# Second layers: TensorE multiplies the mask into banks that are overwritten later, ahead of the fourth scores and ahead of the first convolution input

## What is computed

```python
y_conv = conv_branch(a, a_glu, ...) * silu(z_conv)   # y = a * sigmoid(a_glu); causal depthwise conv, 31 taps;
                                                     # layer norm, silu, 256x256 product
y_mla  = mla_branch(c_q, c_kv, k_rope, ...) * silu(z_mla)   # 8 heads: q, k of 96, v of 64, causal softmax
y_sg   = sgu_branch(u, v, ...) * silu(z_sg)          # gelu(u) * (masked 128x128 mixing of normed gelu(v))
x = x + concat(rms(y_conv), rms(y_mla), rms(y_sg)) @ w_out
```

## Time and profile before

| | |
|---|---|
| median of 3 executions | 1483.45 us (1482.19 to 1486.08) |
| profiled execution | 1483.63 us, of which the span from first to last instruction is 1481.9 us |
| TensorE busy | 1428.2 us, 96% of the span |
| VectorE, ScalarE busy | 986.7 us (67%), 826.7 us (56%) |
| mean granted TensorE clock | 0.988 of full speed |

### The profile page before, as it was taken

One profiled execution on the slowest core, in us unless ns is written; L12 is line 12 of the kernel. 1 busy time (PEld: TensorE's weight loads), 2 busy tenths in 40 slices (PEclk: granted clock), 3 DMA queues, 4 the chain that ended last, 5 costly groups with the idle time before them and its releaser, 6 DMA issues.

```text
span 1481.9 us, 18967 instructions
## 1 busy us (share of the span) xinstructions
PE 1428.2 (96%) x7631; PEld 1203.0 (81%) x7631; DVE 986.7 (67%) x1468; ACT 826.7 (56%) x1337; POOL 44.9 (3%) x72
## 2 busy tenths in 40 slices
PE   7999999999999999989999999999999989899988
PEld 6877888888778888857888888778888878788877
DVE  6665656556766565676765656657656589868984
ACT  6775434445745354464454356765534468856883
POOL 3000000000000000000000000000000020112010
PEclk9999999999999999999999999999999999999999
DMA  9433545554335455423445554424455454424430
GB/s 300 170 114 137 204 171 202 196 171 170 115 125 210 177 190 208 167 90 114 171 175 211 182 186 169 170 105 179 171 201 197 170 156 139 170 101 158 150 115 29
DMA packets 119508, 242.12 MB, mean 163 GB/s; under 512 B 3083, under 2 KB 48957, under 8 KB 119421
## 3 DMA queue, kind: packets, MB, share of 16 engines
q1 hardware_dynamic: 117648, 237.25, 45.1%
q0 software_dynamic: 1408, 3.52, 1.0%
q10 hardware_dynamic: 364, 0.13, 0.0%
HBM read 239.84 MB, written 1.05 MB: 163 GB/s over the span
## 4 chain that ended last, share of the span: by engine, by line
PE 85%; DVE 8%; ACT 5%; issue 1%; DMA 1%; ACTq 0%; DVEq 0%
PE pair L1183 17%; PE pair L1185 17%; PE pair L1184 17%; PE pair L1573 16%; PE pair L1575 8%; PE pair L1338 3%; DVE wlo L1728 2%; PE pair L1281 2%; DVE yacc L2123 2%; PE pair L1359 1%; PE pair L1389 1%; ACT whi L706 1%; PE pair L1344 1%; ACT xparts L747 1%; PE pair L1377 1%
## 5 line engine op out<-in xcount | busy, mean ns | idle before, releaser
L1728 DVE TENSOR_TENSOR wlo<-raw,whi 128x2048 fp32r<-128x2048 f32 (+2 forms) x240 | 504.6, 2132 | 77.4 <-ACT whi L706 76.4
L706 ACT ACTIVATE whi<-raw 128x2048 fp32r<-128x2048 f32 (+2 forms) x238 | 414.5, 1783 | 57.7 <-DMA raw<-in_mlp_w_down 30.5
L1573 PE MATMUL pair<-xparts,whi 128*128 128x512 f32 x1024 | 260.7, 393 | 2.0 <-DVE xparts L1764 1.8
L1183 PE MATMUL pair<-whi,ahi 128*128 128x512 f32 x640 | 253.4, 396 | 1.4 <-DVE alo L1764 1.1
L1184 PE MATMUL pair<-wlo,ahi 128*128 128x512 f32 x640 | 249.9, 390 | 0.0
L1185 PE MATMUL pair<-whi,alo 128*128 128x512 f32 x640 | 249.7, 390 | 0.0
L1183 PE MATMUL pair<-whi,xparts 128*128 128x512 f32 (+2 forms) x624 | 242.2, 388 | 4.5 <-issue 2.6
L1185 PE MATMUL pair<-whi,xparts 128*128 128x512 f32 (+2 forms) x624 | 236.3, 379 | 0.0
L1184 PE MATMUL pair<-wlo,xparts 128*128 128x512 f32 (+2 forms) x624 | 235.7, 378 | 0.0
L1573 PEld LDWEIGHTS pair<-xparts,whi 128*128 128x128 f32 x1024 | 184.1, 189 | 38.6 <-DVE xparts L1764 4.5
L976 ACT ACTIVATE qkv<-pair 128x512 f32<-128x512 f32 x64 | 38.2, 597 | 271.2 <-PE pair L1575 271.2
(11 more groups left out here) (251 smaller groups left out, 1416.1 us busy)
## 6 DMA issues: line engine op xcount, KB each, us to landing
raw<-in_mlp_w_up SPq DMA_DIRECT2D x32, 2048.0 KB, 8.9
raw<-in_mlp_w_down SPq DMA_DIRECT2D x32, 2048.0 KB, 7.5
raw<-in_diff_w_in SPq DMA_DIRECT2D x20, 1024.0 KB, 7.2
raw<-in_w_in SPq DMA_DIRECT2D x10, 2048.0 KB, 8.1
raw<-in_moba_w_in SPq DMA_DIRECT2D x12, 1024.0 KB, 6.1
raw<-in_diff_w_out SPq DMA_DIRECT2D x4, 2048.0 KB, 7.7
raw<-in_w_uq SPq DMA_DIRECT2D x4, 1152.0 KB, 5.5
raw<-in_moba_w_out SPq DMA_DIRECT2D x2, 2048.0 KB, 7.8
```

Of the source, the lines that this page charges most:

```text
L706: act.activation(whi[:, s, cols], raw[:, s, cols], ACT.Copy).then_inc(*t["hi_split"].one())
L1183: pe.matmul(dst, x_hi, w_hi, start=first, stop=False)
L1573: pe.matmul(pair[f % 2][:, f // 2, :], w_hi[:, k, f * P:(f + 1) * P], xparts[:, k, :, :].rearrange("p a n -> p (a n)"), start=k == 0, stop ...
L1728: dve.tensor_tensor(wlo[:, s, cols], raw[:, s, cols], whi[:, s, cols].bitcast(FP32), ALU.subtract)\
```

## The change

A function `keep_busy(bank, times)` issues `times` matmuls of the identity with 256 columns of the causal mask into a bank, each opening and closing its own sum, so nothing is accumulated and what they write is overwritten later. It is called at two places:

- In `scores` for `hp` 3 of both second layers, after `free` has found `pair[0]` emptied and before the wait for the split heads: a new wait until bank 5 is emptied, then 24 matmuls into the second bank of `pair[1]`.
- In `conv_in`, whose two waits change places (the bank first, then `glu_ready`): in the first of the two second layers, 18 matmuls into the first bank of `pair[0]` between the two waits.

```diff
--- before.py
+++ after.py
@@ -103,6 +103,7 @@
 HEAD_PAIRS = 8
 HEADS_PAIR = (1, 2, 3, 3)
 SCORES_APART = 6
+BUSY_CONV, BUSY_SCORES = 18, 24
 VALUES_BLOCK = (1, 2, 4, 5)
 ROPE_BLOCKS = ((0,), (1, 2), (3,), (4, 5))
 SWA_HEADS_BANK = (4, 5, 6, 7)
@@ -1315,10 +1316,19 @@
                             m = pe.transpose(pair[2][0:QK2, part, at:at + P], tile("mla", 2 * hp + c, tt), ident[:, :])
                 m.then_inc(*t.filled[2].one())
 
+            def keep_busy(bank, times):
+
+                for _ in range(times):
+                    pe.matmul(bank[:, 0:2 * P], ident_b[:, :], causal[:, 0:2 * P], start=True, stop=True)
+
             def scores(mixer, hp):
 
                 free(score_pair(mixer, hp))
                 if mixer == "mla":
+                    if hp == 3:
+
+                        pe.wait_ge(*t.emptied[5].now())
+                        keep_busy(pair[1][:, 1, :], BUSY_SCORES)
 
                     pe.wait_ge(*heads_split[hp])
                 elif hp in (0, 4):
@@ -1614,8 +1624,10 @@
                         block_products(layer, n, step[2])
                     elif what == "conv_in":
 
+                        free(0)
+                        if layer == 0:
+                            keep_busy(pair[0][:, 0, :], BUSY_CONV)
                         pe.wait_ge(*t["glu_ready"].after())
-                        free(0)
                         for ct in range(2):
                             for tt in range(TT):
                                 m = pe.transpose(pair[0][:, 0, ct * SEQ + tt * P:ct * SEQ + (tt + 1) * P], conv_tile(ct)(tt),
```

## The result

The changed kernel takes 1476.2 us (median of 5, 1474.38 to 1478.24), beside 1483.45 us before (median of 5 in the same comparison, 1481.12 to 1488.4). The median lies inside the range given, 1475.2 to 1482.3; but the ratio is taken against the kernel before, run beside it, and applied to 1483.45 us it gives 1473.5 us, outside. The direction was right and the gain is nearly double the forecast.

A forecast was written before the change was run, and what follows sets the result against it. TensorE, busy 96% of the span, was taken as the bound, losing time in pauses and half-clock stretches; gains of 2.7 and 2.6 us at the fourth scores, zero at the convolution, took 1483.63 to 1478.3 us, range 1475.2 to 1482.3.

The forecast's parts named there:

- the price: At the fourth scores, 24 mask matmuls stepping by 0.117 us make the true scores about 0.4 us late.
- the sum: Whole kernel: the profiled execution's 1483.63 us, within 0.2 us of the median 1483.45, less 5.3 us gives 1478.3 us.
- The step chain behind the fourth scores: From fourth scores to output projection in both second layers: at full clock the projection starts 2.7 and 2.6 us sooner.
- In the profiled execution there was no drop, so the gain is zero too: At the convolution input: 18 matmuls fit the 3.1 us pause, cost zero, gain zero; up to 5.1 us with a drop.
- if the timed executions of before have drops that the profiled one has not: Listed sign, whole kernel: the forecast is wrong if timed executions of before show clock drops missing from the profiled one.
- The first one's lower side (0.12): Drop at the convolution input before, or fewer in the sliding-window layer after: 1474 to 1477 us; chance 0.12.
- Its upper side (0.20): Drops at the fourth scores in only half of the executions: time near 1481.3 us; chance 0.20.
- The rivals of no change: Fourth scores: a wait takes the gain, or the clock falls anyway, losing 0.4 us per layer, 1484.4 us; chance 0.07.
- a slower kernel: Fourth scores: matmuls not overlapped, 0.283 us each, scores 4.4 us late, 1486.2 us or 1492.4 with the drop; chance 0.06.
- turn 2 at 0.88 us: Behind the fourth scores: the third turning of probabilities takes 0.88 us at full clock instead of 1.49.
- the 0.7 us wait ahead of turn 3: Behind the fourth scores: TensorE, done at about 1297.0, has a short new wait for exponentials; turn 3 starts at 1297.45.
- The wait ahead of mix 3: Behind the fourth scores: a short new wait of TensorE for ScalarE's copy of turn 3, which ends at 1299.95.

The follow-up runs named there:

- b5: The kernel before, unchanged, one more profiled execution: 1491.30 us.
- b4: The kernel before, unchanged, one more profiled execution: 1490.08 us.

## Why the prediction was wrong, point by point

The mechanism was right: both drops behind the fourth scores go, the price is small and everything behind moves up. The size was not, by three terms. The step that failed most is in the sum: that the profiled execution and the median "stand within 0.2 us", so that the drops of one profile could be priced as the drops of all.

- **The step chain behind the fourth scores** was priced at 2.7 and 2.6 us and gives 3.2 and 3.1. One part is the spacing of the mask matmuls. I took 0.117 us from a pair that took 0.40 us, less one duration; the same subtraction over the 24 gives (2.79 - 0.28) / 23 = 0.109, so one pair was too coarse for it. The true scores start (1289.74 - 1287.19) / 24 = 0.106 us each behind the wake, and are 0.1 us late instead of 0.4 (1289.74 - 1286.33 = 3.41 us after the copy begins, 3.31 before). The estimate from the Trainium skill, 0.109 us ("TensorE: Matmul & The Clock Gate", section "Back-to-back issue gap"), which I weighed and left aside, was nearer to that. The other part is ScalarE: its copy of turn 3 starts at 1296.79, while the copies of y 0 still run to 1296.94; I had put the two end to end. Together 0.9 us.
- **"In the profiled execution there was no drop, so the gain is zero too"**, for the convolution input. In three of eight profiles of before there is one, 3.4 us each. The run with the 18 matmuls alone is 1.8 us of means under before and not clear of nothing. At 0.33 us per us at half clock, 3 x 3.4 / 8 is 0.4 us; by VectorE's starts the three drops cost 1.5 to 1.9 us each, 0.6 us on average over the eight. The step is small, but it is not zero.
- **The sum was made against one execution.** That "they stand within 0.2 us" compared the profiled one with a median of three. The mean of 79 is 1485.7, 2.1 us above the profiled one, and its half-clock time is not 20.5 us behind the fourth scores plus a constant. This is the term that was mis-sized most: 6.2 us for the two drops as profiled, and with it the 2.1 us by which the mean of before lies higher and 0.7 us by which that of the changed kernel (1476.7) lies under 1483.63 - 6.2, make the 9.0 us. The prediction listed this itself among the signs of being wrong: "if the timed executions of before have drops that the profiled one has not".

How much of those last 2.8 us belongs to the change? b5 shows that the change can remove more than it did in the first profile: 20.5 and 3.4 us. Over the eight profiles the touched places hold 1.3 + 8.5 + 11.5 = 21.3 us on average, 7.0 us of time by the line. The rest would have to lie elsewhere, where the two programs are the same: 14.1 us in the eight profiles of before, 8.9 us in the changed kernel's executions, 5.2 us or 1.7 us of time apart. The run with 48 matmuls, protected at the same places, has 13.6. VectorE's starts give the touched places directly, without the line: 4.9 to 9.5 us, 6.6 on average, with a 95% interval of about 5.4 to 7.8 from eight profiles. So the touched places' own share is about 7 us. The remaining 2 lie outside them, nearly all ahead of 1190 us, where the two programs do the same: this looks like the luck of the executions, but it is not shown, and stays open.

The rivals. The first one's lower side (0.12) is the one that came nearest: drops at the convolution in some executions of before, and a shorter one in the sliding-window layer in the profile after; the median of 1476.2 lies in its 1474 to 1477. Its upper side (0.20), drops at the fourth scores in only half of the executions, is refuted: all eight profiles have both, though two of the sixteen are only 3.4 us long. That pause is 3.4 us long. The same idea holds elsewhere: the sliding-window layer, with its pause of 2.8 us, had a drop of 3.4 to 10.2 us in all eight (b4 a second one, ahead of the pause), and the 3.1 us of the convolution input had three in eight. So the length of the pause does not decide alone, as the prediction said. The rivals of no change and of a slower kernel fell with the clock at 1.00 and with the 0.106 us a matmul. Of the signs listed, the clock, turn 2 at 0.88 us, the 0.7 us wait ahead of turn 3 and the projection 9.3 us behind the first true scores (9.5 forecast) are in the timeline. The matmuls step by 0.106 us, not 0.117, and end 0.2 us behind the split keys, not 0.4. The wait ahead of mix 3 is not there.

## What to carry to other kernels

Where TensorE pauses and a stretch at 1.2 GHz follows in every profile, filling the pause with useless matmuls that end as the data arrive is worth the stretch, less what the other engines then take. Size the filler by the gap: here 22 and 24 held in every profile, 12 did not always, and 24 more took 0.108 us each, and most of that stayed on the path (2.2 of 2.6 us a layer). Before pricing it, take several profiles, for the stretch comes and goes from execution to execution, and one of them says little about the median; the mean granted clock of each execution shows most of the spread without a profile, the launch aside. The version with two matmuls fewer and one more pause filled has the lowest median of the four timed together, 1475.77 us beside 1477.1 for the changed kernel; with six executions each that is not a clear difference.

## What the runs showed of the hardware

One us at half clock costs 0.33 us here, though TensorE is busy for 96% of the span, and the two profiled drops give 6.2 us for 20.5, 0.30. Behind the fourth scores, against the changed kernel's profile, a drop of 10.2 us cost 2.4 to 3.2 us, one of 3.4 us 1.0, and the one of 20.5 us 7.1. In the run with 12 matmuls a drop began after TensorE had been back at work at full clock for 2.2 us behind the pause (1.8 of them busy). Drops lasted 3.4, 6.8, 10.2 or 20.5 us.
